# Keeping the normed rows in natural order and letting TensorE pick every eighth feature

## The chip, the cores and the metric

The kernel runs on one core of a Trainium2 chip. The metric is the device time of one execution in microseconds (us). The kernel before was timed three times: 981.35, 981.79 and 983.96 us, median 981.79 us. A further, profiled execution took 981.49 us; its span, from the first to the last instruction, is 979.7 us. All rows below are from that one.

## The reference, cut to what matters

One decoder layer over 512 tokens of 1024 features: a modulated RMS norm, token mixers (sparse attention and pooling), an output projection with a residual, a second modulated RMS norm, a mixture of 32 experts of which each token takes 4, a residual and a last norm. The change touches what lies between the second norm and the experts:

```python
h2 = rms_norm(x, norm2_g[l]) * (1.0 + sc2) + sh2          # 512 rows of 1024 features
logits = hf @ w_router + b_router                          # 32 experts, top 4
gu = xb @ w_gu[e] + b_gu[e]                                # per expert, for its tokens
act = gt * jax.nn.sigmoid(SWIGLU_ALPHA * gt) * (up + 1.0)
return act @ w_down[e] + b_down[e]
```

All of this is float32.

## The kernel before, in words

The five engines have a program each, and the order in which every engine issues its work is written out by hand; semaphores join them. Tokens are worked on in four chunks of 128 (`ch`), features in eight groups (`k`, `KD` = 8) of 128. The weights of router and experts are loaded with feature 8q+k in partition q, group k, so that each partition reads one contiguous stretch of memory. The operand that is multiplied with group k must therefore hold the features k, 8+k, 16+k, ... in its 128 partitions.

**Norm and router (340 to 381 us).** VectorE makes the rows of h2: `h2_rows` (L1288) scales X into `natural` (L1291) and adds the shift (L1293). The addition also sorts the features: it writes `h2` (the tile `area_a`) contiguously, in eight runs of 128, and reads both its inputs at every eighth float. TensorE turns each chunk (`h2_turn`, L1724, matmul at L1732): eight transposes of 128x128, the rows as stationary operand (LDWEIGHTS, "PEld" in the rows) and the identity as moving operand. ScalarE copies the turned rows to `h2T` (L963), and TensorE multiplies them with the router's weights (`router`, L1735, recorded at L1523, the helper's line). The `hum` at L1519 is a few matmuls on constants, with no use for the result. GpSimd copies the h2 rows to device memory (L685), `h2_rows` there, 1024 features and 32 weights per token.

**Routing and the first expert (381 to 409 us).** VectorE finds the top 4 and each token's place; TensorE makes the first expert's rows without a gather: a product of `h2` with a one-hot matrix `first` (L1890, 8 groups x 4 chunks of tokens, `h2` stationary 128x128, `first` moving 128x96), which leaves them turned in PSUM. `places` (L1882) gives the token numbers with which GpSimd gathers the rows of the other experts by indirect DMA into `XG` (the tile `apad`, 96 slots of 1056 floats, two buffers).

**Experts (409 to 954 us).** TensorE's order for expert e is: gate and up projection (L1799, L1804, L1810, L1815), down projection of expert e-1 (L1826, L1836), three transposes of e's activations (L1903), and then `turn_rows` (L1791) for expert e+2: eight transposes with a stationary 96x128 from `XG` and the 96x96 identity moving. ScalarE copies those to `xgT` (L993, L994). Sync's queue loads the experts' weights into a ring of 16 pieces of 1 MB, six for each expert; a piece is loaded as soon as TensorE has used the one that lies there. L1564, in the front of the kernel, is a product with 128x128 floats stationary and one column moving.

Of the kernel before, what the change touches and what calls it, by code (L numbers as in the profile page):

```python
# [27 lines left out]
P = 128  # L28
T, D = 512, 1024
C = T // P  # L30
KD = D // P
# [34 lines left out]
def trunk(nc, x, c, norm1_g, norm2_g, w_ada, b_ada, w_in, kv_norm_g, w_uk, w_uv, w_pool, pool_scale,  # L66
          w_a_up, w_b_up, w_out, w_router, b_router, w_gu, b_gu, w_down, b_down, final_g, out,
          slots=SLOTS):
    ctx = ExitStack()
    with ctx:  # L70
        def sb(name, shape, dt=F32):
            return ctx.enter_context(nc.sbuf_tensor(name, shape, dt))

        def sem(name):
            return ctx.enter_context(nc.semaphore(name))
# [18 lines left out]
        ident = sb("ident", [P, P])  # L94
# [33 lines left out]
        ps = ctx.enter_context(nc.psum_tensor("ps", [P, 8, CH], F32))  # L128
# [23 lines left out]
        h2 = area_a[:, :].rearrange("p (c d) -> p c d", c=C)  # L152
# [10 lines left out]
        sh2b = attn[:, 2048:3072]  # L163
# [20 lines left out]
        natural = uvp[:, :, :].rearrange("p a t -> p (a t)")  # L184
        first = natural[:, 0:C * slots].rearrange("p (c s) -> p c s", c=C)
# [14 lines left out]
        XG = apad[:, :, :].rearrange("p g t -> p (g t)").rearrange("p (b d) -> p b d", b=2)  # L200
# [126 lines left out]
        ss3_ok, h2_ok = sem("ss3_ok"), sem("h2_ok")  # L327
# [86 lines left out]
        def merged_part(k, a):  # L414
            return wb_flat[:, buffer_of(("merged", k)), a, 0:T]

        def w_out_part(k, a):
            return wb_flat[:, buffer_of(("merged", k)), a, T:T + CH]
# [23 lines left out]
        def turned(b):  # L442

            return ps[:, b:b + 2, :].rearrange("p b (k s) -> p (b k) s", k=4)[:, :, 0:slots]

        block = ctx.enter_context(nc.Block())

# [616 lines left out]
        def _(dve):  # L1064
            chain = [0]

            def link(ins):

                chain[0] += 1
                ins.then_inc(dve_chain, 1)  # L1070
                dve.wait_ge(dve_chain, chain[0])

            def job(kind, i=0):
                dve.wait_ge(job_done, number[kind, i] + 1)
                return bank(kind, i)

            v = nc.vector
# [43 lines left out]
            for ch in range(C):  # L1121
                b_ = job("tok", ch)
# [123 lines left out]
            for m in range(KD):  # L1246
                b_ = job("B", m)
# [17 lines left out]
            for m in range(KD):  # L1265
# [6 lines left out]
                b_ = job("A", m)  # L1272
# [8 lines left out]
            dve.wait_ge(rows_in, 64)  # L1281
            link(v.scalar_tensor_tensor(out=A2b, in0=A2b, scalar=1.0, in1=n2b, op0=ALU.add, op1=ALU.mult))

            def by_k(row):

                return row.rearrange("p (q k) -> p k q", k=KD)

            def h2_rows(ch):  # L1288
                dve.wait_ge(ss3_ok, ch + 1)
                link(v.reciprocal(rstd3[:, ch:ch + 1], ss3[:, ch:ch + 1]))  # L1290
                link(v.scalar_tensor_tensor(out=natural, in0=X[:, ch, :], scalar=rstd3[:, ch:ch + 1], in1=A2b,  # L1291
                                            op0=ALU.mult, op1=ALU.mult))
                v.tensor_tensor(h2[:, ch, :].rearrange("p (k q) -> p k q", k=KD), by_k(natural), by_k(sh2b),  # L1293
                                ALU.add).then_inc(h2_ok, 1)

            def x1_half(ch, half):

# [11 lines left out]
            for ch in range(C):  # L1309
                if ch:  # L1310
                    h2_rows(ch - 1)
                x1_half(ch, 1)
            dve.wait_ge(by_vec, emptied[number["out", 2 * C - 1]])
            h2_rows(C - 1)


            v.tensor_copy(lg[:, :, 0:NE], job("rt")[:, 0:C * NE].rearrange("p (c e) -> p c e", c=C)).then_inc(by_vec, 1)
            dve.wait_ge(by_vec, emptied[number["rt", 0]])
            for ch in range(C):
                last = v.max(out=m8[:, ch, :], in_=lg[:, ch, 0:NE])  # L1320
# [3 lines left out]
            for ch in range(C):  # L1324
                last = v.match_replace(out=lr[:, ch, :], in_to_replace=m8[:, ch, :], in_values=lg[:, ch, :],
                                       imm_value=TAKEN)
# [13 lines left out]
            b_ = job("rank")  # L1340
# [94 lines left out]
            for ch in range(C):  # L1435
                last = v.scalar_tensor_tensor(out=place31[:, ch:ch + 1], in0=ixa[0:slots, 0, NE - 1:NE], scalar=-float(P * ch),
                                              in1=ixa[0:slots, 1, NE - 1:NE], op0=ALU.add, op1=ALU.add)
            last.then_inc(place_ok, 1)
            dve.wait_ge(place_ok, 1)
            for ch in range(C):  # L1440
                last = v.tensor_scalar(combine[0:slots, ch * P:(ch + 1) * P], iota[0:slots, :], place31[:, ch:ch + 1],
                                       None, ALU.is_equal)
# [7 lines left out]
            with dve.If(most > slots):  # L1450
                with dve.Fori(0, OVER) as r:
# [4 lines left out]
                    with dve.Fori(0, NE) as e:  # L1456
                        n = r * NE + e
                        dve.wait_ge(ov_go, n + 1)
                        for ch in range(C):
                            last = v.tensor_scalar(oh[0][:, 0, ch, :], ranks[:, :], rankm[:, ch, bass.ds(e, 1)], None,  # L1460
                                                   ALU.is_equal)
                        last.then_inc(ov_oh, 1)
                        dve.wait_ge(ov_ix, n + 1)
                        b_ = ps[:, 7, :]
# [36 lines left out]
        def _(pe):  # L1501
            mm = nc.tensor.matmul

            def start(kind, i=0):

                n = number[kind, i]
                if n >= 8:
                    pe.wait_ge(by_act if JOBS[n - 8][2] == "A" else by_vec, emptied[n - 8])
                return bank(kind, i)
# [6 lines left out]
            def hum(b_, times):  # L1516

                for _ in range(times):
                    mm(b_[:, 0:2 * P], onesb[:, :], ones[:, :].bitcast(BF16), start=True, stop=True)  # L1519

            def chain(out_, pairs, done=None, by=1, start_=True):
                for n, (a, b) in enumerate(pairs):
                    last = mm(out_, a, b, start=(n == 0 and start_), stop=(n == len(pairs) - 1))  # L1523
                if done is not None:
                    last.then_inc(done, by)
                return last
# [22 lines left out]
            for i in range(8):  # L1549
                ch, half = i // 2, i % 2  # L1550
                b_ = start("xT", i)
                pe.wait_ge(xn_ok, ch + 1)
                for k in range(4):
                    at = (4 * half + k) * P
                    last = nc.tensor.transpose(b_[:, k * P:(k + 1) * P], xn[:, ch, at:at + P], ident[:, :])
# [37 lines left out]
            b_ = start("uk")  # L1593
            pe.wait_ge(uk_in, 16)
            for i in range(4):
                last = nc.tensor.transpose(b_[:, i * P:(i + 1) * P], uk[:, i * P:(i + 1) * P], ident[:, :])
            last.then_inc(job_done, 1)
            for ch in range(C):
                b_ = start("tr", ch)
# [34 lines left out]
            for h in range(H):  # L1634
                b_ = start("qlat", h)
# [35 lines left out]
            for g in range(NGR):  # L1671
                ch, hh = g // 2, g % 2
                for i in range(4):
                    b_ = start("PT", 4 * g + i)
                    pe.wait_ge(prob_ok, 4 * g + i + 1)
                    for s in range(ch + 1):
                        last = nc.tensor.transpose(b_[:, s * P:(s + 1) * P], Lt[:, i, s * P:(s + 1) * P], ident[:, :])
# [3 lines left out]
                b_ = start("O", g)  # L1681
# [4 lines left out]
                if g == 0:  # L1686
                    pe.wait_ge(pool_in, 16)
                    for i in range(PG):
                        b_ = start("z", i)
                        pe.wait_ge(d_ok, i + 1)  # L1690
                        mm(b_, wpool[:, i, :], dT[:, i, :], start=True, stop=True).then_inc(job_done, 1)
                if hh:
                    b_ = start("V", ch)
                    pe.wait_ge(uv_in, 16 * H)
                    emptied_by("O", g)
                    for a in range(4):
                        last = chain(b_[:, a * P:(a + 1) * P],
                                     [(uvp[:, 2 * a + q, :], o_latT[:, 2 * a + q, :]) for q in range(2)])
# [25 lines left out]
            def h2_turn(ch):  # L1724
                if ch == C - 1:
                    hum(start("h2T", 2 * ch), 5)
                pe.wait_ge(h2_ok, ch + 1)
                for half in range(2):
                    b_ = start("h2T", 2 * ch + half)
                    for k in range(4):  # L1730
                        at = (4 * half + k) * P
                        last = nc.tensor.transpose(b_[:, k * P:(k + 1) * P], h2[:, ch, at:at + P], ident[:, :])  # L1732
                    last.then_inc(job_done, 1)

            def router(ch):  # L1735
# [10 lines left out]
            for k in range(KD):  # L1746
                pe.wait_ge(o_lo_ok, k + 1)
                for ch in range(C):
                    for a, b in ((0, 0), (0, 1), (1, 0)):
                        last = mm(firsts[ch], merged_part(k, a)[:, ch * P:(ch + 1) * P], w_out_part(k, b),  # L1750
                                  start=(k == 0 and a + b == 0), stop=(k == KD - 1 and a == 1))
# [5 lines left out]
            for ch in range(C):  # L1757
                b_ = start("out", 2 * ch + 1)
                w = have("wo", 1)
                for k in range(KD):  # L1760
                    last = mm(b_, mT[:, k, ch * P:(ch + 1) * P], w[:, k, :], start=(k == 0), stop=(k == KD - 1))  # L1761
# [11 lines left out]
            b_ = start("rt")  # L1773
            hum(b_, 4)
            emptied_by("rout", C - 1)
            for ch in range(C):
                last = nc.tensor.transpose(b_[:, ch * NE:(ch + 1) * NE], lgT[:, ch * P:(ch + 1) * P], ident[0:NE, 0:NE])
            last.then_inc(job_done, 1)

            b_ = start("rank")  # L1780
# [8 lines left out]
            def turn_rows(b, done):  # L1789
                for k in range(KD):  # L1790
                    last = nc.tensor.transpose(ps[:, 4 + k // 4, (k % 4) * P:(k % 4) * P + slots],  # L1791
                                               XG[0:slots, b, k * P:(k + 1) * P], ident[0:slots, 0:slots])
                last.then_inc(done, 1)

            def up_wide(b, arrived):
# [91 lines left out]
            pe.wait_ge(first_ok, 1)  # L1887
            for k in range(KD):
                for ch in range(C):
                    last = mm(ps[:, 4 + k // 4, (k % 4) * P:(k % 4) * P + slots], h2[:, ch, k * P:(k + 1) * P], first[:, ch, :],  # L1890
                              start=(ch == 0), stop=(ch == C - 1))
            last.then_inc(tx_done, 1)
            places(0)
# [41 lines left out]
            for ch in range(C):  # L1935
                last = mm(ps[P - NE:P, 7, ch * P:(ch + 1) * P], wts[:, ch, :], ident[:, :], start=True, stop=True,
                          tile_position=(0, P - NE))
# [8 lines left out]
            with pe.If(most > slots):  # L1946
                with pe.Fori(0, OVER) as r:
                    with pe.Fori(0, NE) as e:
                        n = r * NE + e
                        pe.wait_ge(ov_oh, n + 1)  # L1950
                        for ch in range(C):
                            last = mm(ps[0:slots, 7, 0:3], oh[0][:, 0, ch, :], tokid[:, ch, :], start=(ch == 0), stop=(ch == C - 1))
# [19 lines left out]
            for ch in range(C):  # L1972
                for half in range(2):
                    if half:
                        pe.wait_ge(y_ok, NE)
                    last = mm(ps[:, 2 * ch + half, :], combine[:, ch * P:(ch + 1) * P], Y[:, 1, half * CH:(half + 1) * CH],
                              start=True, stop=True)
# [25 lines left out]
```

## Time and profile before

| what | value |
|---|---|
| median of three executions | 981.79 us (981.35 to 983.96) |
| profiled execution, device time | 981.49 us |
| its span | 979.7 us |
| PE busy (matmul) | 941.8 us, 96% |
| PEld busy (weight load) | 505.0 us, 52% |
| DVE busy (VectorE) | 404.6 us, 41% |
| ACT busy (ScalarE) | 227.0 us, 23% |
| POOL busy (GpSimd) | 197.0 us, 20% |

A matmul's record runs from its start to its modelled end, and the records overlap: from a series of n one divides the series' length less one record by n-1 to get the step from one to the next. PEld records overlap with PE records and with one another in the same way.

### The profile page before, as it was taken

What the parts mean: (1) busy time and instruction counts of PE and PEld (TensorE: products, weight loads), DVE (VectorE), ACT (ScalarE), POOL (GpSimd) and SP (SyncE); (2) the same over time, 40 slices, a digit from 0 to 9 for tenths busy, and PEclk for the clock granted to TensorE, in tenths of its full rate; (3) what the DMA queues carried; (4) which work ended last, traced back from release to release, by engine and by line L of the source; (5) the groups of instructions that cost most, each with busy time, mean ns of one, the idle gap of its engine ahead of it and who ended that gap; (6) DMA issues with size and microseconds to landing.
All of it is one profiled execution on the core that took longest, in us unless ns stands there. A gap on an engine that the chain in (4) does not pass through costs nothing.

```text
span 979.7 us, 16888 instructions
## 1 busy us (share of the span) xinstructions
PE 941.8 (96%) x7132; PEld 505.0 (52%) x7132; DVE 404.6 (41%) x835; ACT 227.0 (23%) x488; POOL 197.0 (20%) x240
## 2 busy tenths in 40 slices
PE   4999999999999999999999999999999999999994
PEld 2676666677788748444444444444434444344441
DVE  0484868635534665134323232232423224232245
ACT  6334444443322332111111011110111111011112
POOL 2233931105100001222221112111121211211012
PEclk9999999999999999999999999999999999999998
DMA  9926724520424568999999999999999999999915
GB/s 326 364 92 253 258 87 156 188 86 17 173 86 142 208 251 325 353 353 390 371 341 392 388 380 395 380 394 382 386 390 381 398 374 386 372 382 394 381 34 185
DMA packets 71443, 283.96 MB, mean 290 GB/s; under 512 B 7488, under 2 KB 8796, under 8 KB 54984
## 3 DMA queue, kind: packets, MB, share of 16 engines
q1 hardware_dynamic: 61720, 257.93, 68.2%
q0 software_dynamic: 9648, 24.94, 9.6%
q8 instruction: 58, 0.95, 0.4%
q14 instruction: 17, 0.14, 0.0%
HBM read 272.62 MB, written 18.56 MB: 297 GB/s over the span
## 4 chain that ended last, share of the span: by engine, by line
PE 89%; DVE 4%; ACT 3%; DMA 3%; issue 1%; POOLq 0%; SPq 0%; POOL 0%; DVEq 0%; ACTq 0%
PE ps L1804 22%; PE ps L1523 20%; PE ps L1836 11%; PE ps L1815 11%; PE ps L1826 6%; PE ps L1761 3%; PE ps L1750 2%; PE ps L1791 2%; PE ps L1577 2%; PE ps L1663 2%; PE ps L1544 2%; PE ps L1903 2%; PE ps L1799 1%; DMA X<-in_x_dram 1%; DMA apad<-h_rows,iug 1%
## 5 line engine op out<-in xcount | busy, mean ns | idle before, releaser
L1352 DVE TENSOR_SCALAR mix<-ps 128x384 f32<-128x384 f32 x32 | 17.9, 558 | 344.0 <-ACT attn L998 344.0
L1523 PE MATMUL ps<-h_hi,wb_hl 128*128 128x512 f32 x384 | 125.2, 400 | 0.0
L703 POOL DMA_INDIRECT moe_rows<-mix,ius x31 | 50.9, 1641 | 247.9 <-DVE mix L1401 144.7
L998 ACT ACTIVATE attn<-ps 128x384 f32<-128x384 f32 x32 | 15.7, 491 | 307.0 <-PE ps L1815 307.0
L1523 PEld LDWEIGHTS ps<-h_hi,wb_hl 128*128 128x128 f32 x384 | 72.2, 188 | 20.3 <-issue 5.0
L1523 PE MATMUL ps<-h_lo,wb_hl 128*128 128x512 f32 x192 | 74.8, 389 | 0.0
L1393 DVE SCALAR_TENSOR_TENSOR mix<-ps,WC,attn 32x256 f32<-32x256 f32 x128 | 61.5, 480 | 7.2 <-PE ps L1826 4.9
L1401 DVE SCALAR_TENSOR_TENSOR mix<-ps,WC,attn 64x512 f32<-64x512 f32 x64 | 47.8, 747 | 34.5 <-PE ps L1836 33.5
L1804 PE MATMUL ps<-ring,mix 128*64 128x512 f32 x272 | 59.9, 592 | 0.0
L1804 PE MATMUL ps<-ring,uvp 128*64 128x512 f32 x256 | 56.9, 592 | 0.0
L1836 PE MATMUL ps<-ring,attn 128*64 128x512 f32 x240 | 54.8, 598 | 0.0
L1010 ACT ACTIVATE attn<-ps 128x384 f32<-128x384 f32 x32 | 15.7, 491 | 167.7 <-PE ps L1903 167.7
L622 POOL TENSOR_TENSOR wb_hl<-ring,wb_hl 128x1024 fp32r<-128x1024 f32 x16 | 38.6, 2422 | 78.6 <-ACT wb_hl L837 68.6
L1523 PE MATMUL ps<-zo_hl,wb_hl 128*128 128x512 f32 x192 | 44.9, 390 | 0.0
L1523 PEld LDWEIGHTS ps<-h_lo,wb_hl 128*128 128x128 f32 x192 | 36.1, 188 | 8.6 <-issue 1.7
L1523 PEld LDWEIGHTS ps<-zo_hl,wb_hl 128*128 128x128 f32 x192 | 35.9, 188 | 7.4
L733 POOL COPY ius<-idx 128x1 uint32 (+1 forms) x31 | 5.7, 182 | 157.2 <-DMA moe_rows<-mix,ius 157.2
L1804 PEld LDWEIGHTS ps<-ring,mix 128*64 128x64 f32 x272 | 19.0, 137 | 35.3 <-issue 34.7
L697 POOL DMA_INDIRECT apad<-h_rows,iug x32 | 31.9, 996 | 25.3 <-POOL iug L724 24.4
L1804 PEld LDWEIGHTS ps<-ring,uvp 128*64 128x64 f32 x256 | 17.9, 137 | 33.0 <-issue 32.4
L837 ACT ACTIVATE wb_hl<-ring 128x1024 fp32r<-128x1024 f32 x24 | 25.2, 1053 | 39.6 <-PE ps L1523 32.6
L1836 PEld LDWEIGHTS ps<-ring,attn 128*64 128x64 f32 x240 | 15.9, 136 | 31.9 <-issue 31.9
(308 smaller groups left out, 1521.1 us busy)
## 6 DMA issues: line engine op xcount, KB each, us to landing
ring<-in_w_gu_dram SPq DMA_DIRECT2D x66, 1024.0 KB, 16.7
ring<-in_w_down_dram SPq DMA_DIRECT2D x30, 1024.0 KB, 12.3
ring<-in_w_ada_dram SPq DMA_DIRECT2D x12, 2048.0 KB, 11.2
area_b<-in_w_gu_dram SPq DMA_DIRECT2D x16, 1024.0 KB, 15.5
hT<-in_w_gu_dram SPq DMA_DIRECT2D x16, 1024.0 KB, 16.3
X<-in_w_gu_dram SPq DMA_DIRECT2D x16, 1024.0 KB, 15.6
area_a<-in_w_gu_dram SPq DMA_DIRECT2D x14, 1024.0 KB, 16.7
ring<-in_w_in_dram SPq DMA_DIRECT2D x6, 2048.0 KB, 8.5
```

What stands on the lines that cost most here:

```text
L622: nc.gpsimd.tensor_tensor(wb_hl[:, buffer_of(BLOCKS[n]), 1, :, :], block_w(n), wb_hl[:, buffer_of(BLOCKS[n]), 0, :, :], ALU.subtract).then ...
L697: pool.indirect_dma_start(out=XG[0:slots, b, :], out_offset=None, in_=h2_dram, in_offset=bass.IndirectOffsetOnAxis(ap=iug[0:slots, b:b + 1 ...
L703: pool.indirect_dma_start(out=y_dram, in_=Y[0:slots, b, :], in_offset=None, out_offset=bass.IndirectOffsetOnAxis(ap=which, axis=0), bounds ...
L837: nc.scalar.activation(wb_hl[:, buffer_of(BLOCKS[n]), 0, :, :], block_w(n), ACT.Copy).then_inc(b_hi_ok, 1)
L1393: v.scalar_tensor_tensor(out=Y[SA:slots, b, sl], in0=ps[SB * j:SB * (j + 1), at + 1, 0:2 * P], scalar=WC[SA:slots, w:w + 1], in1=g2b[SA:sl ...
L1401: v.scalar_tensor_tensor(out=Y[0:SA, b, sl], in0=ps[SA * g:SA * (g + 1), at, :], scalar=WC[0:SA, w:w + 1], in1=g2b[0:SA, sl], op0=ALU.mult ...
L1523: last = mm(out_, a, b, start=(n == 0 and start_), stop=(n == len(pairs) - 1))
L1761: last = mm(b_, mT[:, k, ch * P:(ch + 1) * P], w[:, k, :], start=(k == 0), stop=(k == KD - 1))
L1804: mm(ps[SA * g:SA * (g + 1), 0, :], xgT[b][:, k, 0:SA], w[:, k % 2, g, :, :, :], start=False, stop=(k == KD - 1), tile_position=(0, SA * g))
L1815: last = mm(ps[SB * j:SB * (j + 1), 1, 0:2 * P], xgT[b][:, k, SA:slots], w[:, k % 2, j // 2, j % 2, :, :], start=False, stop=(k == KD - 1) ...
L1826: last = mm(ps[SB * j:SB * (j + 1), at + 1, 0:2 * P], actT[:, 2, SB * k:SB * (k + 1)], w[:, k % 2, 2 * P * j:2 * P * (j + 1)], start=(k == ...
L1836: last = mm(ps[SA * g:SA * (g + 1), at, :], actT[:, k % 2, SA * (k // 2):SA * (k // 2) + SA], w[:, k % 2, g * CH:(g + 1) * CH], start=(k = ...
```

## The change

`h2` keeps the natural order of features: VectorE's addition reads and writes contiguously. The rows in device memory and the gathered rows are in natural order too. The sorting is done where TensorE loads its stationary operand: the transposes of `h2` and of `XG`, and the one-hot product, name the features k, 8+k, 16+k, ... (a step of 8 floats, 32 bytes) as the 128 columns of the stationary operand. Their number, shapes, results in PSUM and order are what they were. `turn_rows` is also called by the branch for an expert with over 96 tokens.

```diff
+        def by_k(row):
+            return row.rearrange("p (q k) -> p k q", k=KD)
+
         block = ctx.enter_context(nc.Block())
...
-            def by_k(row):
-
-                return row.rearrange("p (q k) -> p k q", k=KD)
-
             def h2_rows(ch):
...
-                v.tensor_tensor(h2[:, ch, :].rearrange("p (k q) -> p k q", k=KD), by_k(natural), by_k(sh2b),
-                                ALU.add).then_inc(h2_ok, 1)
+                v.tensor_tensor(h2[:, ch, :], natural, sh2b, ALU.add).then_inc(h2_ok, 1)
...
                     for k in range(4):
-                        at = (4 * half + k) * P
-                        last = nc.tensor.transpose(b_[:, k * P:(k + 1) * P], h2[:, ch, at:at + P], ident[:, :])
+                        last = nc.tensor.transpose(b_[:, k * P:(k + 1) * P], by_k(h2[:, ch, :])[:, 4 * half + k, :],
+                                                   ident[:, :])
...
             def turn_rows(b, done):
                 for k in range(KD):
                     last = nc.tensor.transpose(ps[:, 4 + k // 4, (k % 4) * P:(k % 4) * P + slots],
-                                               XG[0:slots, b, k * P:(k + 1) * P], ident[0:slots, 0:slots])
+                                               by_k(XG[0:slots, b, 0:D])[:, k, :], ident[0:slots, 0:slots])
...
-                    last = mm(ps[:, 4 + k // 4, (k % 4) * P:(k % 4) * P + slots], h2[:, ch, k * P:(k + 1) * P], first[:, ch, :],
+                    last = mm(ps[:, 4 + k // 4, (k % 4) * P:(k % 4) * P + slots], by_k(h2[:, ch, :])[:, k, :], first[:, ch, :],
                               start=(ch == 0), stop=(ch == C - 1))
```

## Rows read from the trace of the kernel before

**Rows 1.** The page's chain that ended last, by engine and by line
```profile
PE 89%; DVE 4%; ACT 3%; DMA 3%; issue 1%; POOLq 0%; SPq 0%; POOL 0%; DVEq 0%; ACTq 0%
PE ps L1804 22%; PE ps L1523 20%; PE ps L1836 11%; PE ps L1815 11%; PE ps L1826 6%; PE ps L1761 3%; PE ps L1750 2%; PE ps L1791 2%; PE ps L1577 2%; PE ps L1663 2%; PE ps L1544 2%; PE ps L1903 2%; PE ps L1799 1%; DMA X<-in_x_dram 1%; DMA apad<-h_rows,iug 1%
```

**Rows 2.** Windows, 420 to 800 us: us, busy (count) by engine, PEclk, DMA share, GB/s
```profile
420.00:600.00 180.00, 180.00 (x1734) 78.09 (x1734) 59.87 (x99) 21.31 (x54) 35.32 (x43) 1.00 1.01 377
600.00:800.00 200.00, 200.00 (x1836) 83.31 (x1830) 61.10 (x108) 23.17 (x59) 32.89 (x46) 1.00 1.02 388
```

**Rows 3.** Waits of SP's queue, 420 to 950 us: us in total, times, longest
```profile
SPq L489 <- PE ps L1815: 260.8, 57, 9.2
SPq L485 <- PE ps L1836: 127.2, 55, 4.9
```

**Rows 4.** Chain in order of time, 600 to 625 us: start, us, what
```profile
604.64 0.48 PE ps L1903 x3
605.12 0.66 PE ps L1791 x8
605.78 0.34 PE ps L1799 x2
...
621.97 0.48 PE ps L1903 x3
622.45 0.66 PE ps L1791 x8
```

**Rows 5.** VectorE by form: busy us, mean ns, idle before
```profile
L1293 DVE TENSOR_TENSOR area_a<-uvp,attn 128x1024 f32<-128x1024 f32 x4 | 8.1, 2037 | 0.1
L1220 DVE TENSOR_TENSOR wb_hl<-ring,wb_hl 128x1024 fp32r<-128x1024 f32 x8 | 9.8, 1226 | 29.0 <-ACT wb_hl L837 29.0
```

**Rows 6.** Timeline, 360 to 378 us: start, us, engine, instruction, idle before
```profile
361.49 1.91 PE L1732 MATMUL ps<-ident,area_a 128*128 128x128 f32 x16
370.20 1.93 PE L1523 MATMUL ps<-hT,wr 128*32 128x128 f32 x16
372.06 0.85 PEld L1732 LDWEIGHTS ps<-ident,area_a 128*128 128x128 f32 x8 [0.20 <-issue]
373.08 3.68 PE L1523 MATMUL ps<-hT,wr 128*32 128x128 f32 x32
374.85 2.03 DVE L1293 TENSOR_TENSOR area_a<-uvp,attn 128x1024 f32<-128x1024 f32 x1
376.70 0.72 PE L1519 MATMUL ps<-ones,onesb 128*128 128x256 bf16 x5
377.15 0.91 PEld L1732 LDWEIGHTS ps<-ident,area_a 128*128 128x128 f32 x8
377.25 1.04 PE L1732 MATMUL ps<-ident,area_a 128*128 128x128 f32 x8
```

**Rows 7.** PEld by form: busy us, mean ns, idle before
```profile
L1791 PEld LDWEIGHTS ps<-ident,apad 96*128 96x128 f32 x248 | 23.1, 140 | 2.2 <-DMA apad<-h_rows,iug 1.8 <-issue 0.4
L1890 PEld LDWEIGHTS ps<-uvp,area_a 128*128 128x128 f32 x64 | 7.2, 192 | 0.5 <-DVE uvp L1378 0.5
L1732 PEld LDWEIGHTS ps<-ident,area_a 128*128 128x128 f32 x32 | 3.6, 141 | 0.7 <-issue 0.7
L1564 PEld LDWEIGHTS ps<-ones,mix 128*128 128x128 f32 x32 | 4.0, 191 | 2.1 <-issue 0.8 <-ACT hT L816 0.8 <-ACT mix L811 0.3
```

**Rows 8.** PE's timeline, 26 to 60 us: the product with one moving column
```profile
38.13 1.05 PE L1564 MATMUL ps<-ones,mix 128*128 128x1 f32 x8
```

**Rows 9.** PE's timeline, 385 to 410 us
```profile
386.26 7.38 PE L1890 MATMUL ps<-uvp,area_a 128*128 128x96 f32 x64 [0.18 <-DVE uvp L1378]
393.48 1.56 PE L1882 MATMUL ps<-tokid,attn 128*96 128x3 bf16 x32
394.98 0.41 PE L1799 MATMUL ps<-maskb,chosen 96*64 96x512 bf16 x2
407.26 0.88 PE L1791 MATMUL ps<-ident,apad 96*128 96x96 f32 x8 [1.34 <-DMA apad<-h_rows,iug]
```

## The prediction, as put on record before the result

> **What bounds the kernel now.** I read the chain that ended last first. It is TensorE for 89% of the span, and `turn_rows`, the eight transposes of L1791, is a link of it with 2% [rows 1]. That is the line to follow: 248 of the changed loads are there. Then the windows over the experts. The matmul column equals the window's length, 180.00 of 180.00 us and 200.00 of 200.00 us, at a granted clock of 1.00 [rows 2]. The DMA share is about 1.0 as well, so one must ask which of the two is late. The waits of SP's queue answer: the loads wait for TensorE to free a piece, 260.8 us and 127.2 us in total [rows 3], never the other way round. So whatever TensorE's own stream takes longer per expert there is added to the time, and nothing on VectorE or GpSimd counts. In the chain in order of time the transposes stand without a gap between L1903 and the next expert's L1799: 0.66 us for eight, 82 ns each, in every expert [rows 4].
>
> **Part 1: VectorE's addition.** Before, it reads two operands at a step of 32 bytes: 2037 ns, four times. The nearest contiguous row, also a tensor_tensor of 128x1024 from two SBUF operands, takes 1226 ns [rows 5]. So each gets 0.81 us shorter. What is that worth? The last of the four is the one that matters: it ends at 374.85+2.03 = 376.88 us. But TensorE, which reads h2 next, is busy with the router's products of two other chunks from 373.08 to 376.76 and with five filler matmuls to about 377.25, where the transposes start [rows 6]. That work hides the addition already, with some 0.3 us to spare. Chunk 1 and 2 are ready before their transposes as well: the sixteen of chunk 0 and 1 run at a step of (1.91-0.27)/15 = 109 ns, and chunk 2's start at 372.06, right behind the router's first product, which ends then [rows 6]. I cost the gain at 0. If the cover were gone it would be 0.8 us, once. GpSimd's copies of h2 start 0.8 us earlier, and nobody waits for these.
>
> **Part 2: the stationary operand at a step of 32 bytes.** The counts are 31 x 8 = 248 transposes of gathered rows, 64 loads of the one-hot product and 32 transposes of h2 [rows 7]. Nothing else on TensorE, and no DMA, is added or moved. The question is only how long a strided load takes, and how much of it lies beneath the matmul ahead of it.
>
> First the slack. The product with a single moving column has nothing to stream, so its step is the load's: (1.05-0.25)/7 = 114 ns for 128x128 floats [rows 8] (0.25 us is one record of it). The one-hot product has the step (7.38-0.28)/63 = 113 ns, though it streams 96 columns [rows 9]: the same as with one column, so it is bound by its loads and has **no slack**. The load of a transpose has a shorter record, 140 against 192 ns [rows 7]; the 51 ns less are about half of the 114, as if the plain product read its operand twice and the transpose once. I take 60 ns for a transpose's load. The transposes of gathered rows have a step of 82 ns: 22 ns of slack. Those of h2, 109 ns: 49 ns of slack.
>
> Now the price. No row shows a strided load on TensorE. The nearest row is VectorE's: its additional time is (2037-1226)/1024 = 0.79 ns per element with two strided streams [rows 5]. Shared over the two streams that is 0.40 ns for each strided element, 51 ns for 128 columns, which would nearly double a transpose's load, to 111 ns. From it:
> - Gathered rows: 60+51-82 = 29 ns for each but the first of a turn, whose load is beneath L1903's matmul. 31 x 7 x 29 ns = 6.3 us, all on the chain.
> - One-hot product: two readings, 2 x 51 = 102 ns, 63 times: 6.4 us. It is on the path as well: `places`, the token numbers, the gather and the next loads stand behind it. Against it, 1.34 us of TensorE's wait for the gather at 407.26 [rows 9] can be eaten up if the delayed gather meets less traffic; I take none of it.
> - h2's transposes: 60+51 = 111 against 109 ns: under 0.1 us.
>
> Sum: 12.8 us, and 981.49 + 12.8 = 994.3 for the profiled execution. Its time is 0.3 us under the median of the runs shown, so I say **994.5 us**, 1.3% slower.
>
> The ends. Below: a strided load costs nothing and the addition's gain shows, -0.8 us; a gain for a strided load itself I exclude, since the same number of columns is loaded. Above: VectorE's reads of two streams may run side by side, and then each strided element costs the whole 0.79 ns, 102 ns for each reading. The gathered rows then take 60+102-82 = 80 ns x 217 = 17.4 us, the one-hot product 204 ns x 63 = 12.9 us, h2's transposes 53 ns x 28 = 1.5 us: 31.8 us. The farthest end takes VectorE's whole 2037/1024 = 1.99 ns per element as the price of a strided read: a reading of 255 ns, and 173 x 217 + 397 x 63 + 146 x 28 ns = 66.6 us. I take the first since TensorE has one strided stream and not two, and because half of the extra time for half of the streams is what that row says directly.
>
> The Trainium skill bears on it (SBUF — State Buffer, the note on cachelines): a read that goes to a new 16-byte line with each element pays, and two hits per line are wanted to hide the access. A step of 32 bytes is a new line for each float. VectorE's 2037 ns agree with it; whether it holds for TensorE's loads no row here shows. If "two hits" were taken as a factor of 2, the estimate is a load of 120 instead of 60 ns, and 8.2 + 7.2 + 0.3 = 15.7 us. The skill also gives a load as columns divided by 1.2 GHz (TensorE: Matmul & The Clock Gate, LDWEIGHTS), an estimate of 107 ns for 128 columns. The trace disagrees: 82 ns from one transpose to the next, each with such a load. If it were right, any doubling would cost twice what I say.
>
> **The rivals.**
> - **A. TensorE's loads don't mind the step: not slower.** Place: all 344 loads. For it: TensorE has to fetch far faster than VectorE in any case, so its path may be another one than VectorE's; up to 82 ns the transposes would show nothing. Against it: the addition's 2037 ns. It decides if a strided load stays at 60 ns; the one-hot product's step would stay at 113 ns. Then the time is the median less 0 to 0.8 us: 981.4 us.
> - **B. My forecast:** 51 ns for each reading, 994.5 us.
> - **C. The whole of VectorE's extra time for one stream:** 981.8 + 31.8 = 1013.6 us. For it: the two streams of VectorE could well be read side by side. Against it: a load would then have to take 162 ns, almost three times the contiguous one.
> - **D. Half-hidden:** the load grows by up to 22 ns and the transposes of the experts hide it, but the one-hot product can't. 2 x 22 x 63 = 2.8 us, 984.6 us. It needs a penalty much lower than VectorE's.
> - **E. Faster:** the earlier h2 and the moved gathers let the routing stage start earlier than TensorE's fillers allow. Nothing in rows 6 speaks for more than 0.8 us.
>
> **How the numbers follow.** B 0.50, A 0.28, C 0.11, D 0.08, E 0.03. About 0.3%, 2.9 us, is what a measurement of this kernel can tell from no change. B, C and all but a little of D are slower by over that: 0.67. A and the rest of D are within it: 0.30. Faster: 0.03. B's own range is 989 to 1001 (a penalty of 40 to 65 ns for each reading, with or without the two readings in the one-hot product). The range must reach down to A, so 980.8; above it ends at 1003, which leaves out C and the far end, a little over 1 in 10.
>
> **What the changed profile would show.** L1293 at about 1.23 us instead of 2.04 (if not, the rewrite does not do what it says). The step of L1890: 113 ns says A, about 215 says B, over 300 says C; this is the cleanest sign, as it has no slack. L1791 for eight: 0.66 us says A or D, 0.86 us B, 1.2 us C, and the period of an expert grows by the same amount. L1799 right behind it, with no wait for ScalarE's copy, says that only the transposes were stretched. Wrong would be the whole account if L1791 kept its 82 ns and the time rose, or if TensorE showed waits in the experts' windows.

## The result, and the profile after

The changed kernel takes 1000.19 us, median of four executions (997.0 to 1000.47), against 982.33 us for the kernel before on the same chip: 1.0175 of it, 95% interval 1.0162 to 1.0188. The forecast was 994.5 us and slower; the time lies in the stated range, 5.7 us above the forecast. The profiled execution took 997.0 us, the shortest of the four, with a span of 995.2 us.

First the experts, in the windows view (columns as in [rows 2]) and in SP's waits. The kernel is TensorE's as before, and the loads still wait for TensorE [rows 2, 3].

```profile
420.00:600.00 180.00, 180.00 (x1704) 78.82 (x1703) 59.49 (x98) 19.81 (x50) 34.19 (x40) 1.00 1.00 372
600.00:800.00 200.00, 200.00 (x1812) 85.32 (x1812) 57.47 (x101) 23.15 (x59) 33.87 (x47) 1.00 1.02 388
```
```profile
SPq L492 <- PE ps L1813: 286.1, 60, 10.7
SPq L488 <- PE ps L1834: 133.4, 56, 4.9
```

The count of matmuls in such a window (1812, before 1836) depends on where the window cuts an expert, and doesn't give the loss: the run with the turns alone, below, has 1871 in the same 200 us, and its turns take as long as these. The chain in order of time gives it. L1791 is L1789 now:

```profile
617.71 0.48 PE ps L1901 x3
618.19 0.86 PE ps L1789 x8
619.05 0.34 PE ps L1797 x2
...
635.24 0.48 PE ps L1901 x3
635.72 0.86 PE ps L1789 x8
```

Eight transposes take 0.86 us where they took 0.66 [rows 4]; their neighbours, L1901 and L1797, are what they were, and so is everything else of an expert. The period is 635.72-618.19 = 17.53 us, before 17.33. That is 0.20 us for a turn.

The loads by form (busy us, mean ns, idle before), and VectorE's addition, which is L1292 now:

```profile
L1789 PEld LDWEIGHTS ps<-ident,apad 96*128 96x128 f32 x248 | 29.9, 202 | 0.8 <-issue 0.8
L1888 PEld LDWEIGHTS ps<-uvp,area_a 128*128 128x128 f32 x64 | 15.3, 335 | 0.5 <-DVE uvp L1376 0.5
L1562 PEld LDWEIGHTS ps<-ones,mix 128*128 128x128 f32 x32 | 3.9, 191 | 1.8 <-ACT hT L819 0.8 <-issue 0.8
L1729 PEld LDWEIGHTS ps<-ident,area_a 128*128 128x128 f32 x32 | 3.9, 192 | 0.7 <-issue 0.7
```
```profile
L1292 DVE TENSOR_TENSOR area_a<-uvp,attn 128x1024 f32<-128x1024 f32 x4 | 4.9, 1225 | 0.1
```

A transpose's load record grew from 140 to 202 ns, the one-hot product's from 192 to 335 ns, and the untouched L1562 stayed [rows 7]. The addition fell from 2037 to 1225 ns, as it should [rows 5].

The routing stage, TensorE's timeline; it answers to [rows 9]. `places`, the bias matmuls (L1799 before) and the first series of gate and up are L1880, L1797 and L1802 now:

```profile
386.45 15.55 PE L1888 MATMUL ps<-uvp,area_a 128*128 128x96 f32 x64 [0.18 <-DVE uvp L1376]
401.80 2.69 PE L1880 MATMUL ps<-tokid,attn 128*96 128x3 bf16 x32
404.42 0.64 PE L1797 MATMUL ps<-maskb,chosen 96*64 96x512 bf16 x2
404.84 5.06 PE L1802 MATMUL ps<-area_b,mix 128*64 128x512 f32 x16
409.74 3.60 PE L1802 MATMUL ps<-ring,mix 128*64 128x512 f32 x16
419.51 0.55 PE L1901 MATMUL ps<-ident,attn 128*128 128x128 f32 x3 [1.44 <-DVE attn L1355]
```
And its windows:
```profile
386.00:390.00 4.00, 3.82 (x18) 3.55 (x16) 3.89 (x10) 0.00 (x0) 0.19 (x1) 1.00 1.02 424
390.00:400.00 10.00, 10.00 (x44) 10.00 (x44) 1.18 (x1) 0.00 (x0) 0.58 (x1) 0.54 0.31 129
400.00:410.00 10.00, 10.00 (x61) 6.26 (x62) 1.11 (x8) 0.90 (x2) 2.46 (x4) 0.61 0.68 242
```

Two things are to be seen. The product takes 15.55 us instead of 7.38: its step is (15.55-0.44)/63 = 240 ns, before 113. And the granted clock, which the kernel before keeps at 1.00 from 386 to 410 us, falls to one half, 1.2 GHz, from about 391 to 408 us, four microseconds into the product. Three pieces of work behind the product run into that: `places` takes 2.69 us instead of 1.56, the bias matmuls 0.64 instead of 0.41, and of two equal series of sixteen at L1802 the first takes 5.06 us and the second, back at 2.4 GHz, 3.60.

From start to start, before to after, the time of expert 1's first matmul moved by 10.86 us (409.13 to 419.99). Of this the product has 8.13, `places` 1.12, the two bias matmuls 0.19, the series of sixteen 1.46, the stage ahead 0.19, and the rest gives 0.23 back. The 30 turns behind it add 5.95: the last but one down projection, TensorE's last work on the chain, ends at 968.47 us instead of 951.66, 16.8 us later. The 31st turn, the first in time, costs nothing: behind it TensorE waits for VectorE at the transposes of the activations, 0.42 us before and 1.44 us after. VectorE waits there for ScalarE, and ScalarE stands behind a read of the gathered rows and a table load. In the kernel before:

```profile
404.63 0.20 ACT L1002 ACTIVATE WC<-apad 96x1 f32<-96x1 f32 x1 [10.05 <-DMA apad<-h_rows,iug]
404.85 1.28 ACT L998 ACT_TABLE_LOAD   x1
```

So the gather is only just on the path: from the end of L1815 to the transposes of the activations it is 2.64 us before and 2.50 after, where the gather is early enough. That is the larger part of the 0.23 us. The remaining tail of this execution is 1.3 us shorter than before's; in a second profile of the changed kernel (below) it is 0.2 us longer, so the tail is scatter, and 16.8 us plus scatter is the loss.

### The profile page after: what moved, and what is told of

The parts are those of the page before. It is cut to its first block, busy times and chain, and to the rows that moved or that the text cites. A ratio compares the mean times of both kernels' runs of the same rounds, so it can differ in the third digit from the quotient of the medians.

```text
span 995.2 us, 16888 instructions
## 1 busy us (share of the span) xinstructions
PE 959.2 (96%) x7132; PEld 522.5 (53%) x7132; DVE 400.6 (40%) x835; ACT 226.9 (23%) x488; POOL 196.9 (20%) x240
## 4 chain that ended last, share of the span: by engine, by line
PE 92%; DVE 4%; DMA 2%; ACT 1%; issue 1%; SPq 0%; POOLq 0%; DVEq 0%; ACTq 0%
PE ps L1802 22%; PE ps L1521 20%; PE ps L1834 11%; PE ps L1813 11%; PE ps L1824 5%; PE ps L1759 3%; PE ps L1789 3%; PE ps L1748 2%; PE ps L1542 2%; PE ps L1575 2%; PE ps L1661 2%; PE ps L1888 2%; PE ps L1901 1%; DMA ring<-in_w_ada_dram 1%; PE ps L1797 1%
## 5 line engine op out<-in xcount | busy, mean ns | idle before, releaser
L1350 DVE TENSOR_SCALAR mix<-ps 128x384 f32<-128x384 f32 x32 | 17.9, 558 | 351.2 <-ACT attn L1001 351.2
L1001 ACT ACTIVATE attn<-ps 128x384 f32<-128x384 f32 x32 | 15.7, 490 | 309.6 <-PE ps L1813 309.6
L1802 PE MATMUL ps<-ring,mix 128*64 128x512 f32 x272 | 59.9, 592 | 0.0
L1802 PE MATMUL ps<-ring,uvp 128*64 128x512 f32 x256 | 56.9, 592 | 0.0
L1013 ACT ACTIVATE attn<-ps 128x384 f32<-128x384 f32 x32 | 15.7, 490 | 168.7 <-PE ps L1901 168.7
L1802 PEld LDWEIGHTS ps<-ring,mix 128*64 128x64 f32 x272 | 19.0, 137 | 35.3 <-issue 34.7
L1802 PEld LDWEIGHTS ps<-ring,uvp 128*64 128x64 f32 x256 | 17.9, 137 | 33.0 <-issue 32.4
## 6 DMA issues: line engine op xcount, KB each, us to landing
area_a<-in_w_gu_dram SPq DMA_DIRECT2D x14, 1024.0 KB, 15.4
```

The costliest lines, as they stand in the source:

```text
L1802: mm(ps[SA * g:SA * (g + 1), 0, :], xgT[b][:, k, 0:SA], w[:, k % 2, g, :, :, :], start=False, stop=(k == KD - 1), tile_position=(0, SA * g))
```

## The experiments

**Each part alone.** Three kernels, each with one part of the change; the kernel before, run beside them, took 982.79 us. The first and the second are the kernel before with one part put in (`every_8th` is `by_k` under another name). The first:

```diff
-                                               XG[0:slots, b, k * P:(k + 1) * P], ident[0:slots, 0:slots])
+                                               every_8th(XG[0:slots, b, 0:D])[:, k, :], ident[0:slots, 0:slots])
```

> The kernel before, with the step of 8 floats in the 248 transposes of gathered rows alone (h2 stays sorted, so experts 1 to 31 get their features in the wrong order; the amount of work is the same). Theory (a strided load takes about 107 ns for 128 columns, and only what exceeds the matmul's 82 ns shows): eight transposes 0.86 us instead of 0.66, 31 x 0.20 = 6.2 us slower than before, with the clock at 1.00 from 390 to 420 us and no wait of TensorE in the experts. Rival (most of the loss is in the routing stage and the turns are partly hidden): under 3 us slower.

988.88 us (987.74 to 988.99), 1.0058 [1.0036, 1.0081] of before: +6.1 us between the medians (3.5 to 8.0 by the interval). The clock stays at 1.00 from 386 to 410 us, and the chain in order of time has the turn at 0.86 us:

```profile
590.79 0.48 PE ps L1906 x3
591.26 0.86 PE ps L1794 x8
592.12 0.34 PE ps L1802 x2
```

From expert 1's first matmul to the end of the last but one down projection it takes 548.4 us, before 542.5: the turns cost 5.9 us here too, and the rival, under 3 us, falls. The second:

```diff
-                    last = mm(ps[...], h2[:, ch, k * P:(k + 1) * P], first[:, ch, :],
+                    last = mm(ps[...], every_8th(h2[:, ch, :])[:, k, :], first[:, ch, :],
```

> The kernel before, with the step of 8 floats in the 64 loads of the one-hot product alone (expert 0 gets its features in the wrong order). Theory (two readings of 119 ns per load, no slack, and the clock falls in the middle of the product because the array waits for loads): product 15.5 us instead of 7.4, granted clock 0.5 from some 391 to 408 us, 10.7 to 14 us slower than before, with the spread between executions that the changed kernel has. Rival (loads alone, the half clock costs nothing since the product is bound by loads): 8 us slower, and no spread.

991.99 us (991.36 to 993.63), 1.0100 [1.0076, 1.0124]: +9.2 us. The timeline is the changed kernel's: the product and, behind it, the first series slowed by the half clock and the second not.

```profile
386.14 15.58 PE L1893 MATMUL ps<-uvp,area_a 128*128 128x96 f32 x64 [0.18 <-DVE uvp L1381]
404.56 5.40 PE L1807 MATMUL ps<-area_b,mix 128*64 128x512 f32 x16
409.80 3.60 PE L1807 MATMUL ps<-ring,mix 128*64 128x512 f32 x16
420.04 0.41 PE L1802 MATMUL ps<-maskb,chosen 96*64 96x512 bf16 x2
```

The granted clock is 0.56 from 390 to 400 us and 0.59 from 400 to 410. In the trace expert 1 starts 10.9 us later than before; in the medians the loss is 9.2 us, somewhat under the 10.7 I had expected, but the interval (7.5 to 12.2 us) holds both. The rival's 8 us lies in the interval as well, and the spread, 2.3 us, is no larger than the 4.1 us of the kernel before, so it is the trace and not the time that speaks against the rival. The third is the changed kernel, with its contiguous addition and its strided transposes of h2, and without the other two:

```diff
-                                               by_k(XG[0:slots, b, 0:D])[:, k, :], ident[0:slots, 0:slots])
+                                               XG[0:slots, b, k * P:(k + 1) * P], ident[0:slots, 0:slots])
-                    last = mm(ps[...], by_k(h2[:, ch, :])[:, k, :], first[:, ch, :],
+                    last = mm(ps[...], h2[:, ch, k * P:(k + 1) * P], first[:, ch, :],
```

> The changed kernel with its contiguous addition and its strided transposes of h2, but the one-hot product and the transposes of gathered rows read contiguously as before (all experts get their features in the wrong order, the router the right one). Theory: within 0.5 us of before: the 0.81 us of each addition is hidden by TensorE, and the 32 strided loads fit beneath matmuls of 107 ns. The rival that the addition's gain can be had: 0.8 us or more faster.

981.25 us, 0.9987 [0.9977, 0.9997]: 1.5 us between the medians, 0.13% by the ratio, faster and just beyond the interval. That is more than I had allowed, and more than the 0.8 us that the last addition alone could give. The trace doesn't show it as the additions': from the first transpose of h2 to the start of the product it takes 24.89 us, before 24.77, and from expert 1's first matmul to the end of the last but one down projection 542.5 us as before. The last experiment below, which has the same contiguous addition, does not repeat it. The three ratios add up to 1.0145 and the changed kernel's is 1.0175; the intervals of the parts are wide enough for that difference. The traces say it more sharply. From the product's start to expert 1 the changed kernel takes 33.55 us and the product alone 33.91 (before 22.87), and behind it the changed kernel takes 548.5 us, the turns alone 548.4 and the product alone 542.5: the parts add up within some 0.4 us.

**The changed kernel again.** No edit; beside more runs of the kernel before.

> The changed kernel once more. Two parts alone gave +6.1 and +9.2 us, the third -1.5 us, in all 13.8 us, where the changed kernel had 17.9 us over its own runs of before. Theory (the parts add up, and the rest is how long the half clock lasts behind the product in an execution): 996 to 1000.5 us, the slower executions with the lower granted clock, mean ratio to before 1.015 to 1.018. Rival (the parts add more together than alone): all executions at 1000 us.

999.46 us (997.93 to 1000.48) against 982.16 us, 1.0170 [1.0151, 1.0188]: 17 us once more. The profiled execution has the same pieces within 0.2 us, with the end of the last but one down projection at 969.32 us. The granted clock of the five executions is 0.984, 0.984, 0.984, 0.982 and 0.984, and the one at 0.982 is not the only long one (1000.34 us, beside 1000.48 at 0.984), so the spread is not the clock's alone. The rival falls with the one at 997.93.

**Keeping the clock up.** The changed kernel with fillers in the product:

```diff
                               start=(ch == 0), stop=(ch == C - 1))
+                    if (k, ch) != (KD - 1, C - 1):
+                        hum(bank("ix", 0), 1)
```

> The changed kernel with one filler matmul (bf16, 256 columns, into a bank that is not in use) behind each of the first 63 matmuls of the one-hot product. Theory (the clock falls because the array stands still during the strided loads, and that costs 2.8 us or more behind the product): the fillers go beneath the loads, the product stays at 15 to 16 us, the granted clock stays 1.00 through 390 to 408 us, and the time is 2.5 to 6 us below the changed kernel's, with little spread. Rival 1 (the fillers' own loads and columns add up): product 22 us, 6 us slower than the changed kernel. Rival 2 (the half clock costs nothing): the time of the changed kernel.

The product has 32 matmuls, each of which leaves two loads and two records in the trace, so there are 31 fillers and not 63. The windows, and TensorE behind the product:

```profile
390.00:400.00 10.00, 10.00 (x55) 10.00 (x56) 0.89 (x1) 0.00 (x0) 0.30 (x1) 1.00 0.27 111
400.00:410.00 10.00, 10.00 (x78) 7.01 (x80) 1.11 (x8) 0.90 (x2) 2.46 (x4) 1.00 0.49 172
```
```profile
403.49 0.61 PE L1888 MATMUL ps<-uvp,area_a 128*128 128x96 f32 x2
403.94 1.56 PE L1880 MATMUL ps<-tokid,attn 128*96 128x3 bf16 x32
405.43 0.41 PE L1797 MATMUL ps<-maskb,chosen 96*64 96x512 bf16 x2
405.67 3.60 PE L1802 MATMUL ps<-area_b,mix 128*64 128x512 f32 x16
```

The clock stays at 1.00, and `places`, the bias and the first series are back at 1.56, 0.41 and 3.60 us. The loads are strided as before and the only new thing is work in the gaps. So the fall came from the array standing still beneath the strided loads, and the half clock cost these 2.8 us. But the fillers weren't free: from one pair of records to the next it is 555 ns instead of 2 x 240, and the product, from its start to that of `places`, takes 17.8 us instead of 15.4. From the product's start to expert 1 it comes to 33.65 us, against 33.55 and 33.72 in the two profiles of the changed kernel: nothing gained. The time is 998.97 us (996.66 to 999.34), 1.0166 [1.0144, 1.0189] of before, 1.2 us below the changed kernel's, which the scatter doesn't tell from nothing, and with a spread of 2.7 us that isn't the little I had expected. The mechanism was right; the product's size and the gain were wrong: a remedy that costs what it gives.

**Which steps cost.** The kernel before with another step for each expert's turn and each group of the product, and six additions on VectorE ahead of the residual:

```diff
+        def stepped(row, k, s):
+            per = D // (P * s)
+            at = (k // s) % per * P * s + k % s
+            return row[:, at:at + (P - 1) * s + 1:s]
...
-                                               XG[0:slots, b, k * P:(k + 1) * P], ident[0:slots, 0:slots])
+                                               stepped(XG[0:slots, b, 0:D], k, s), ident[0:slots, 0:slots])
...
-                    last = mm(ps[...], h2[:, ch, k * P:(k + 1) * P], first[:, ch, :],
+                    last = mm(ps[...], stepped(h2[:, ch, :], 0, k + 1), first[:, ch, :],
...
-                turn_rows(e % 2, tx_done)
+                turn_rows(e % 2, tx_done, e % 8 + 1)
```

> The kernel before with other steps, features out of order: the transposes for expert e read their rows at a step of e mod 8 + 1 floats (1 to 8), the one-hot product's group k at a step of k+1 floats; and six more additions of 128x1024 on VectorE ahead of the residual: both inputs contiguous, one at a step of 8, both at 8, the output at 8, both inputs at 4, both at 2. Theory 1 (a line of 16 bytes: two floats of each line are enough): a load's record stays at 141 and 192 ns for steps 1 and 2 and is at its full 206 and 335 ns from step 4 on, step 3 in between. Theory 2 (it grows with the bytes passed over): 8 floats are worse than 4. For VectorE theory 1 and the price in the prediction (half of the extra time for each stream): one strided input 1.63 us, two 2.04 us, steps of 4 like 8, steps of 2 like contiguous. Rival: one strided input costs as much as two.

VectorE by form: L1288 has all three operands contiguous, L1289 one input at a step of 8 floats, L1290 both, L1291 the output, L1292 both inputs at 4, L1293 both at 2.

```profile
L1289 DVE TENSOR_TENSOR uvp<-attn 128x1024 f32<-128x1024 f32 x1 | 2.0, 2032 | 0.0
L1290 DVE TENSOR_TENSOR uvp<-attn 128x1024 f32<-128x1024 f32 x1 | 2.0, 2024 | 0.0
L1291 DVE TENSOR_TENSOR uvp<-attn 128x1024 f32<-128x1024 f32 x1 | 2.0, 2024 | 0.0
L1292 DVE TENSOR_TENSOR uvp<-attn 128x1024 f32<-128x1024 f32 x1 | 2.0, 2019 | 0.0
L1293 DVE TENSOR_TENSOR uvp<-attn 128x1024 f32<-128x1024 f32 x1 | 1.2, 1228 | 0.0
L1288 DVE TENSOR_TENSOR uvp<-attn 128x1024 f32<-128x1024 f32 x1 | 1.2, 1225 | 0.0
```

The kernel took 1006.6 us, a number of no further use. One strided stream costs as much as two, so the price in my expectation falls and its rival stands. The product's loads (count, then shortest, median and longest record in ns, first and last start), from windows in order of time. The step grows by one float every eight loads; a window at the border of two steps holds both:

```profile
L1901 PEld LDWEIGHTS ps<-uvp,area_a x12: 186/192/197, 396.6 to 397.9; 128*128 128x128 f32 x12
L1901 PEld LDWEIGHTS ps<-uvp,area_a x9: 196/197/263, 397.9 to 399.0; 128*128 128x128 f32 x9
L1901 PEld LDWEIGHTS ps<-uvp,area_a x7: 261/261/317, 398.8 to 399.9; 128*128 128x128 f32 x7
L1901 PEld LDWEIGHTS ps<-uvp,area_a x5: 317/330/330, 399.9 to 400.8; 128*128 128x128 f32 x5
...
L1901 PEld LDWEIGHTS ps<-uvp,area_a x5: 334/335/337, 407.8 to 408.8; 128*128 128x128 f32 x5
```

192 ns at step 1, 197 at 2, 261 at 3, 330 at 4, and it stays at 314 to 337 up to 8. This product begins with contiguous loads, and here the granted clock fell only some 9 us into it (1.00 from 400 to 405 us, 0.70 from 405 to 407, 0.50 from 407 to 416). The turns, in the chain in order of time, for experts 7 (step 8), 8 (step 1), 9 (step 2) and 13 (step 6):

```profile
521.26 0.86 PE ps L1802 x8
538.78 0.66 PE ps L1802 x8
556.12 0.93 PE ps L1802 x8
...
626.46 1.05 PE ps L1802 x8
```

For VectorE and the product theory 1 holds and theory 2 falls: a step of 2 floats, two of each 16 bytes, is free (for the product's loads but for 5 ns); from 4 floats the price is full. For the transposes neither holds: a step of 2 already costs, 0.93 us, more than the changed kernel's 8, and the worst of all is 6 (steps 3, 4, 5 and 7 take 0.90, 0.94, 0.90 and 0.96 us).

**No strided read at all.** The kernel before, natural order, with the weights loaded in natural order too:

```diff
-            gu = w_gu[0, bass.ds(e, 1), :, :].rearrange("a (p k) n -> p (a k n)", k=KD)
-            return gu[:, q * PAIR:(q + 1) * PAIR]
+            gu = w_gu[0, bass.ds(e, 1), :, :].rearrange("a (k p) n -> p (a k) n", k=KD)
+            return gu[:, 2 * q:2 * q + 2, :]
...
-                v.tensor_tensor(h2[:, ch, :].rearrange("p (k q) -> p k q", k=KD), by_k(natural), by_k(sh2b),
-                                ALU.add).then_inc(h2_ok, 1)
+                v.tensor_tensor(h2[:, ch, :], natural, sh2b, ALU.add).then_inc(h2_ok, 1)
```

> The kernel before with natural order throughout and no strided read at all: the addition is contiguous, and the router's and the gate/up weights are loaded with feature 128k+p in partition p, group k, instead of 8p+k, so that a piece's rows per partition are two stretches of 4 KB instead of one of 8 KB. Theory (the loss is all in strided loads, and VectorE's gain is hidden): within 2 us of before. Rival 1 (the shorter stretches make the weights late, since the DMA share is already 1.0): TensorE waits for pieces in the experts, some per cent slower. Rival 2 (VectorE's 0.8 us counts): 0.8 us faster.

981.77 us (twelve executions, 980.57 to 983.89), 0.9995 [0.9983, 1.0007] of before. SP's waits:

```profile
SPq L489 <- PE ps L1814: 201.6, 53, 9.1
SPq L485 <- PE ps L1835: 102.4, 49, 4.8
```

The weights take longer to land (18.4 us for a gate/up piece in the ring's first slots, before 16.7), and SP waits less for TensorE than in [rows 3], but it still waits for it and not the other way round: TensorE is busy for 180.00 of 180.00 us from 420 to 600 us and for 200.00 of 200.00 from 600 to 800, so rival 1 falls. Rival 2's 0.8 us lies within the interval, and it is the trace that speaks against it: from the first transpose of h2 to the product's start it takes 24.78 us, before 24.77. So natural order by itself costs nothing and gains nothing that these runs can tell; no version here beats the kernel before by more than 0.13%, and that one's gain the trace doesn't place.

## Why the prediction was right, point by point

- **The bound.** Right: the experts are TensorE's, and 30 of the 31 turns pay in full. I had all 31 on the chain; the first in time is followed by a wait for VectorE and pays nothing.
- **The addition.** Right: 0.81 us shorter each. The filler matmuls and the router's products still set the start of the last transposes of h2, 377.44 us against 377.25 [rows 6], and in the version without strided reads this stage is no shorter.
- **Gathered rows.** Forecast 6.3 us, trace 5.95 us in 30 turns, alone 5.9 us in the trace and 6.1 between the medians. The step of a strided transpose was put at 111 ns, and a turn of eight at 82 + 7 x 111 = 860 ns, which is the 0.86 us measured.
- **The one-hot product.** Forecast 102 ns more for each load, measured 240-113 = 127: 8.1 us instead of 6.4. Its place and its lack of slack were right, its price a fifth too low. (What I took for two readings of one load are the two loads of a float32 matmul at full length: 32 matmuls, 64 loads of 113 ns; the count was the same.)
- **h2's transposes.** Forecast under 0.1 us, found 0.12 us from the first of them to the product's start (24.89 against 24.77 us).
- **What was missing: the clock.** The working had the product stretched and all else as it was: what runs behind the product was put at no change, without a look at the clock. A product that waits for its loads leaves the array still for a good part of each step, and the clock fell some four microseconds into it. It cost 2.8 us, not in the product but behind it, and the fillers' run shows that it was this.
- **The gather.** I left 1.34 us that might be given back. Nearly none was: the wait for VectorE stands right behind it, TensorE waits 1.44 us there after instead of 0.42, and 0.14 us are left as gain. In the run with the turns alone the gather landed later, and from the end of L1815's work to the transposes of the activations it is 3.55 us. That scatter of 0.9 us belongs to no part of the change.
- **The sum.** Forecast 12.8 us, 17.9 us between the medians, 16.8 us in the trace to the last but one down projection. What lies between 12.8 and 16.8 is the product's price (+1.7), the clock (+2.8), the turns (-0.35), h2's transposes (under +0.1) and what was given back (-0.2). The time still fell into the range of the forecast because the range was wide above; the clock was not among the reasons for its width.
- **Why the price is what it is.** Here the argument was wrong though the number was near, and that was luck. I halved VectorE's 0.79 ns per element, as if two strided streams shared a cost. One stream costs VectorE the same as two, so by my own reasoning the price should have been the whole 0.79 ns, 102 ns a reading, and rival C's 1013.6 us. TensorE's loads show no fixed cost per element either: 127 ns for 128 columns in the product, some 50 ns in a transpose. What the two have in common is a factor of about 2 on the load (113 to 240 ns; some 57 to 111 ns, if a transpose's contiguous load is half of the plain one, which is an inference and was not measured by itself). The factor of 2 in the estimate drawn from the Trainium skill (SBUF — State Buffer, the note on cachelines) gave 15.7 us and was nearer than my price, in part by luck: it was near for the product (7.2 us, measured 8.1), too high for the turns (8.2, measured 5.95), and had no clock in it. Of its rule that two hits per line are needed for full speed, the trace agrees for VectorE and the plain load (free at two floats of a line, full price at one) and disagrees for the transpose, where two floats of a line cost as well.
- **A page's load time.** I set the Trainium skill's columns divided by 1.2 GHz (TensorE: Matmul & The Clock Gate, LDWEIGHTS), 107 ns for 128 columns, aside for all loads. The plain float32 load's 113 ns are near it. The transposes' steps of 82 ns disagree, and so does `places` at full clock: 96 columns of bf16 would be 80 ns by it, and the step is 45 ns.

## What to carry to other kernels

Read from the trace which loads of TensorE have slack beneath their matmuls before making them slower: a load's step with a one-column matmul, beside the step of the series in question, says it. In these runs a float32 product that waits for its loads took about twice as long once its stationary operand was read at every fourth float or wider, and eight transposes took 0.86 to 1.05 us instead of 0.66 at every step from 2 floats on. Sort the rows once on an engine that has time, as this kernel did, or lay the other operand out in natural order, which was free here. And when a change makes a series on TensorE wait for its loads, look at the granted clock of what runs behind it: here that was 2.8 us.

## What the runs showed that I had not expected

The product's strided load does not care about the granted clock; contiguous loads do. The product's load records (count, shortest, median and longest in ns) at a granted clock of 1.00, 388 to 390 us, and of 0.50, 398 to 400 us, in the changed kernel:

```profile
L1888 PEld LDWEIGHTS ps<-uvp,area_a x10: 334/335/336, 387.9 to 390.0; 128*128 128x128 f32 x10
...
L1888 PEld LDWEIGHTS ps<-uvp,area_a x10: 334/335/341, 397.9 to 400.0; 128*128 128x128 f32 x10
```

Ten loads take the same 2.1 us at both. `places`, with contiguous bf16 loads of 96 columns and only three columns moving, goes from (1.56-0.18)/31 = 45 ns a step to (2.69-0.22)/31 = 80 at half clock. For contiguous float32 loads the run with the steps has a row at either level: transposes of h2, the first line at 1.00, the second at 0.50.

```profile
L1743 PEld LDWEIGHTS ps<-ident,area_a x8: 137/141/143, 364.0 to 364.7; 128*128 128x128 f32 x8
L1743 PEld LDWEIGHTS ps<-ident,area_a x8: 183/231/231, 370.4 to 371.7; 128*128 128x128 f32 x8
```

So the product itself lost nothing to the throttle, which is why its stretch did not show the clock; only the windows did. A transpose's strided load also depends on the step in a way that no line of 16 bytes explains (0.93 us for eight at a step of 2 floats, 1.05 at 6, 0.86 at 8); why, these runs leave open.
